# An encoder layer whose last tiles are finished another way: a reordered tail, and four row tiles whose residual is added by an accumulating transfer

## The chip, the cores and the metric

The kernel runs on one core of one Trainium2 chip. The metric is the device time of one execution in microseconds (us). Three runs of the kernel before gave 1161.38, 1163.57 and 1164.84 us, a median of 1163.57. One further execution was profiled: it took 1163.79 us, of which the profile's span covers 1162.1.

## The reference

One layer of a transformer-like encoder over 1024 tokens of width 1024, in float32:

```
h = x + rms_norm(Mix(rms_norm(x, g_pre_mix)), g_post_mix)
u = rms_norm(h, g_pre_mlp)
f = square(relu(u @ w_ff_in))          # 1024 x 4096
y = f @ w_ff_out                        # 1024 x 1024
out = h + rms_norm(y, g_post_mlp)       # y * rsqrt(mean(y*y) + EPS) * g + h
```

Mix is one input projection, three groups of heads (stick-breaking attention, a gated recurrence, windowed attention) and an output projection. The change touches only the last line: how `h` is kept meanwhile and how the last norm and the last addition are made.

## The kernel before

The tokens lie in 8 tiles of 128 rows (`TOK`); `y[:, i, :]` is tile i, 128 partitions by 1024 columns of float32 (512 KB). After Mix, `y` holds `h`. The MLP needs `y`'s space, so SyncE writes each tile of `h` to a DRAM tensor `h_dram` (`h_spill` in the profile) around 483 to 506 us, and reads all of it back into `h_back` at 1050 us, 4 MB in one transfer.

The MLP is cut into 8 stages (`STAGES`): even ones make hidden columns, odd ones add their share to `y`. A stage is 7 products of 512x512x512 blocks (Strassen-like; `P1, P2, P6, P5, P7, P3, P4`, in this order). Each float32 product is three passes of rounded parts: ScalarE (ACT) rounds the operands to `a_op` and `b_op` (`round_operands`), VectorE (DVE) makes what is left of them (`rest_operands`), TensorE (PE) multiplies, and DVE adds the product in PSUM (`ps`) to its one or two blocks of `y` (`evict_output`). In the last stage P2 ends the block of tiles 0 to 3 and columns 0 to 511, P7 ends the block of tiles 4 to 7 and columns 512 to 1023, P3 ends tiles 0 to 3, columns 512 to 1023, and P4 ends tiles 4 to 7, columns 0 to 511. P4 is made tile by tile, so that each of its four tiles can be taken when it is done (`last_tile_sum`).

The tail that follows, all written out by hand in the order of each engine's queue:

- ACT squares and sums half rows (`late_squares`): eight halves that are done early into `sumsq_b`, then for each tile the other half into `sumsq`, followed by Ln and Exp that give a first `rs0` of the tile's reciprocal root.
- DVE multiplies every half row by the gain (`gained_half`, 16 of them into `out_gained`), turns `sumsq_b` into `var_b`, adds P4's tiles, improves the root (`final_rsqrt`, four small instructions for one to four tiles) and makes `y = out_gained * rstd + h_back` (`final_tile`, 8 of them).
- SyncE's queue (SP) sends each finished tile to `out`, 512 KB each, and waits for all of them.
- GpSimd (POOL) does nothing after 500 us.

`out_gained` lies over the weight blocks `wq21`, `wq12` and so on; `junk_late`, the squares' unused output, lies over `a_sum`.

Of the kernel before, what the change touches and what calls it, by code (L numbers as in the profile page):

```python
# [19 lines left out]
ALU = mybir.AluOpType  # L20
ACT = mybir.ActivationFunctionType
AX_X = mybir.AxisListType.X

P = 128
BANK = 512
# [13 lines left out]
TOK = S // P  # L39
# [24 lines left out]
PRODUCTS = 7  # L64
# [19 lines left out]
def encoder_layer(nc, x, g_pre_mix, w_in, conv_w, conv_b, lru_wa, lru_ba, lru_wx, lru_bx,  # L84
# [5 lines left out]
    with ExitStack() as ctx:  # L90
# [16 lines left out]
        def sem(name):  # L107
            return ctx.enter_context(nc.semaphore(name))
# [137 lines left out]
        half_done, product_done = sem("half_done"), sem("product_done")  # L246
        act_evicted, dve_evicted = sem("act_evicted"), sem("dve_evicted")
        f_relu, f_ready, sums_ready = sem("f_relu"), sem("f_ready"), sem("sums_ready")
        var_b_ready = sem("var_b_ready")
        h_loaded, out_gain_done, out_ready, out_stored = (  # L250
            sem("h_loaded"), sem("out_gain_done"), sem("out_ready"), sem("out_stored"))
        act_step, dve_step, pool_step = sem("act_step"), sem("dve_step"), sem("pool_step")
# [124 lines left out]
        def halves(s, i):  # L377

            return 2 * (PRODUCTS * s + i) + 2
# [17 lines left out]
        def dve_reads(n):  # L397

            count = 0
            for s, i in (divmod(m, PRODUCTS) for m in range(n)):  # L400
                if i in (P2, P3, P4, P7):
                    count += 2
                if s % 2 and s > 1 and i in (P1, P6, P5, P7):
                    count += 2
            return count
# [25 lines left out]
        def _(sp):  # L431
# [89 lines left out]
            sp.dma_start(wq11[:, :, :], block_of(0, 0, 0)).then_inc(wq_loaded[0], 16)  # L521
            for i in range(TOK):
                sp.wait_ge(h_ready, i + 1)
                sp.dma_start(h_dram[P * i:P * (i + 1), :], y[:, i, :]).then_inc(h_stored[i // 4], 16)
                if i == 3:
                    sp.dma_start(wq21[:, :, :], block_of(0, 1, 0)).then_inc(wq_loaded[2], 16)
                if i == 7:
                    sp.dma_start(wq12[:, :, :], block_of(0, 0, 1)).then_inc(wq_loaded[1], 16)
                    sp.dma_start(wq22[:, :, :], block_of(0, 1, 1)).then_inc(wq_loaded[3], 16)
# [12 lines left out]
            for half in range(2):  # L542
                sp.wait_ge(h_stored[half], 16 * 4)
            sp.wait_ge(a_lo_ready, halves(STAGES - 2, P4))
            sp.dma_start(h_back[:, :, :], h_dram.rearrange("(i p) d -> p i d", p=P))\
                .then_inc(h_loaded, 16)
            for i in range(TOK):
                sp.wait_ge(out_ready, i + 1)
                sp.dma_start(out[0, P * i:P * (i + 1), :], y[:, i, :]).then_inc(out_stored, 16)
            sp.wait_ge(out_stored, 16 * TOK)  # L550


        N_CONST_LOADS = 10
# [2 lines left out]
        def _(pool):  # L556
# [80 lines left out]
            for i in range(TOK - 1):  # L637
                pool.wait_ge(y_added, banks_out(3) + 2 * (i + 1))
                nc.gpsimd.tensor_tensor(y_gained[:, i, :], y[:, i, :], rs_row[:, :], ALU.mult)\
                    .then_inc(y_gain_done, 1)  # L640

        @block.tensor
# [381 lines left out]
        def _(act):  # L1026
# [268 lines left out]
            def turned(half):  # L1295

                for k in range(0, KD, 2):
                    t = KD * half + k
                    act.wait_ge(xt_ready, 2 * KD + t + 1)
                    nc.scalar.activation(ut[:, half, k, :], ps[:, 4 + t % 4, :], ACT.Copy,  # L1300
                                         scale=g_pre_mlp_c[:, k:k + 1]).then_inc(ut_by_act, 1)
# [75 lines left out]
            def relu_squared(s, i):  # L1377

                f = {P2: f11, P7: f22, P3: f12, P4: f21}[i]
                act.wait_ge(dve_evicted, dve_reads(PRODUCTS * s + i + 1))  # L1380
                n_relu[0] += 1
                nc.scalar.activation(f[:, :, :], f[:, :, :], ACT.Relu).then_inc(f_relu, 1)
                act.wait_ge(f_relu, n_relu[0])
                nc.scalar.activation(f[:, :, :], f[:, :, :], ACT.Square).then_inc(f_ready, 1)
# [10 lines left out]
            normed(1)  # L1395
            round_operands(1)
            turned(1)
            for n in range(N_PRODUCTS):
                s, i = divmod(n, PRODUCTS)
                if n:  # L1400
                    evict(n - 1)
                    if n + 1 < N_PRODUCTS:
                        round_operands(n + 1)
                if s % 2 == 0 and i in (P6, P3, P4):
                    relu_squared(s, i - 1 if i != P6 else P2)
                if s % 2 and i == P1:
                    relu_squared(s - 1, P4)

            def late_squares(i, c, total):

                n_squares[0] += 1
                act.wait_ge(sumsq_ready, n_squares[0] - 1)
                nc.scalar.activation(junk_late[:, BANK * c:BANK * (c + 1)],
                                     y[:, i, BANK * c:BANK * (c + 1)], ACT.Square,
                                     accum_out=total[:, i:i + 1]).then_inc(sumsq_ready, 1)

            last = PRODUCTS * (STAGES - 1)
            act.wait_ge(a_lo_ready, halves(STAGES - 1, P4))
            act.wait_ge(dve_evicted, dve_reads(last + P7 + 1))
            for i in range(TOK):  # L1420
                late_squares(i, i // 4, sumsq_b)
            act.wait_ge(sumsq_ready, n_squares[0])
            for i in range(TOK):
                act.wait_ge(dve_evicted, dve_reads(last + P3) + i // 2 + 1 if i < 4
                            else dve_reads(last + P3 + 1) + i - 3)
                late_squares(i, 1 - i // 4, sumsq)
                act.wait_ge(var_b_ready, 1)
                act.wait_ge(sumsq_ready, n_squares[0])
                after(nc.scalar.activation(ln_var[:, i:i + 1], sumsq[:, i:i + 1], ACT.Ln,
                                           scale=1.0 / D, bias=var_b[:, i:i + 1]))  # L1430
                nc.scalar.activation(rs0[:, i:i + 1], ln_var[:, i:i + 1], ACT.Exp, scale=-0.5)\
                    .then_inc(rs0_ready, 1)


        @block.vector
        def _(dve):
# [436 lines left out]
            def evict(n):  # L1873
# [3 lines left out]
                else:  # L1877
                    evict_hidden(n, s, i)


            SUMS_AT = (("S1", "T2", "S2"), ("T3",), ("S3",), ("S4",), ("T4",), (), ("T1",))

# [7 lines left out]
            for n in range(N_PRODUCTS):  # L1890
                s, i = divmod(n, PRODUCTS)
                if n:
                    if i != P2:
                        rest_operands(n + 1, [0])
                    evict(n - 1)
                    rest_operands(n + 1, range(2) if i == P2 else [1])
                for name in SUMS_AT[i]:
                    if name == "T1":
                        if s + 1 < STAGES:
                            block_sum(s + 1, name)  # L1900
                    elif name != "S1" or s % 2:
                        block_sum(s, name)


            def gained_half(i, c):

                cols = slice(BANK * c, BANK * (c + 1))
                nc.vector.tensor_tensor(out_gained[:, i, cols], y[:, i, cols], rs_row[:, cols],  # L1908
                                        ALU.mult).then_inc(out_gain_done, 1)

            def final_tile(i):

                nc.vector.scalar_tensor_tensor(out=y[:, i, :], in0=out_gained[:, i, :],  # L1913
                                               scalar=rstd[:, i:i + 1], in1=h_back[:, i, :],
                                               op0=ALU.mult, op1=ALU.add).then_inc(out_ready, 1)
# [12 lines left out]
            def last_tile_sum(t):  # L1928

                n = N_PRODUCTS - 1  # L1930
                dve.wait_ge(product_done, 2 * n + t + 1)
                n_evicted[0] += 1
                nc.vector.tensor_tensor(y[:, 4 + t, 0:BANK], y[:, 4 + t, 0:BANK],
                                        ps[:, 4 * (n % 2) + t, :], ALU.add)\
                    .then_inc(dve_evicted, 1)
                dve.wait_ge(dve_evicted, n_evicted[0])
                gained_half(4 + t, 0)

            dve.wait_ge(rows_loaded, 32)
            dve.wait_ge(sumsq_ready, 4 * TOK)  # L1940
            nc.vector.tensor_scalar(var_b[:, :], sumsq_b[:, :], 1.0 / D, EPS, ALU.mult, ALU.add)\
                .then_inc(var_b_ready, 1)
            dve.wait_ge(dve_evicted, n_evicted[0])
            for i in range(4):
                gained_half(i, 0)
            for i in range(4, TOK):
                gained_half(i, 1)
            for i in range(4):
                gained_half(i, 1)
            last_tile_sum(0)  # L1950
            last_tile_sum(1)
            dve.wait_ge(h_loaded, 16)
            dve.wait_ge(var_b_ready, 1)
            final_rsqrt(range(4), 1)
            dve.wait_ge(out_gain_done, 14)
            final_tile(0)
            final_tile(1)
            last_tile_sum(2)
            final_rsqrt((4, 5), 2)
            final_tile(2)  # L1960
            last_tile_sum(3)
            final_tile(3)
            final_tile(4)
            final_tile(5)
            for i in (6, 7):
                final_rsqrt((i,), i - 3)
                if i == 6:
                    dve.wait_ge(out_gain_done, 16)
                final_tile(i)


# [20 lines left out]
```

## Time and profile before

| | |
|---|---|
| median of three runs | 1163.57 us (1161.38 to 1164.84) |
| the profiled execution | 1163.79 us, span 1162.1 us |
| PE busy | 1082.9 us, 93% of the span |
| DVE busy | 808.2 us, 70% |
| ACT busy | 574.1 us, 49% |
| POOL busy | 76.2 us, 7% |
| chain that ended last | PE 84%, DVE 8%, ACT 4%, issue 2%, DMA 1% |
| stores of `out` | 8 of 512 KB, median 2.7 us from issue to landing |

The shares are means over the whole span. What the change is worth is read from the last 35 us, where the engines take turns.

### The profile page before, as it was taken

How to read it: one execution, taken by the hardware profiler on the slowest of the kernel's cores; microseconds unless marked ns; L12 is line 12 of the kernel's file. 1: busy time of each engine (PE TensorE's matmuls, PEld its weight loads, DVE VectorE, ACT ScalarE, POOL GpSimd, SP SyncE). 2: the span in 40 equal slices, each digit the busy share in tenths (PEclk: the TensorE clock that was granted, in tenths of full speed). 3: DMA queues.
4: the chain of work that ended last, by engine and by line, in shares of the span. 5: the costliest groups of instructions: out<-in, count | busy, mean ns of one | idle time of the engine just before them, and what ended most of it. 6: DMA issues, size and time to landing. Idle time of an engine off the chain costs nothing.

```text
span 1162.1 us, 12115 instructions
## 1 busy us (share of the span) xinstructions
PE 1082.9 (93%) x4844; PEld 844.6 (73%) x4844; DVE 808.2 (70%) x767; ACT 574.1 (49%) x705; POOL 76.2 (7%) x69
## 2 busy tenths in 40 slices
PE   6999999997899999849999999999999999999992
PEld 5777777875535458637888888878888878888781
DVE  2536657655464645767778777789876898867988
ACT  6313433357464540475665546654366533467443
POOL 0004113201101000400000000000000000000000
PEclk9999999978899999978999999999999999999996
DMA  7211112110000122160130311301303013025003
GB/s 220 76 46 37 37 37 73 37 37 1 1 1 1 36 108 93 48 225 1 37 109 1 111 34 37 109 1 38 108 1 143 2 37 109 1 76 214 1 1 144
DMA packets 44624, 70.44 MB, mean 61 GB/s; under 512 B 10228, under 2 KB 19736, under 8 KB 44568
## 3 DMA queue, kind: packets, MB, share of 16 engines
q1 hardware_dynamic: 43528, 69.66, 17.6%
q8 instruction: 39, 0.64, 0.2%
q10 hardware_dynamic: 1040, 0.00, 0.1%
q14 instruction: 17, 0.14, 0.0%
HBM read 61.27 MB, written 8.39 MB: 60 GB/s over the span
## 4 chain that ended last, share of the span: by engine, by line
PE 84%; DVE 8%; ACT 4%; issue 2%; DMA 1%; SPq 1%; DVEq 0%; ACTq 0%
PE ps L648 25%; PE ps L652 24%; PE ps L650 24%; PE ps L864 2%; PE ps L877 1%; PE ps L724 1%; PE ps L832 1%; PE ps L892 1%; PE ps L787 1%; DVE sb_e L1658 1%; ACT sb_e L1233 1%; DVE y L1913 1%; DMA g_pre_mix_c<-in_g_pre_mix 1%; ACT sb_w L1213 1%; DVE out_gained L1908 1%
## 5 line engine op out<-in xcount | busy, mean ns | idle before, releaser
L648 PE MATMUL ps<-a_op,b_op 128*128 128x512 f32 x448 | 175.9, 393 | 5.4 <-DVE b_op L1800 4.5
L648 PE MATMUL ps<-b_op,a_op 128*128 128x512 f32 x448 | 174.6, 390 | 2.7 <-issue 2.7
L650 PE MATMUL ps<-a_op,b_op 128*128 128x512 f32 x448 | 175.6, 392 | 0.0
L652 PE MATMUL ps<-a_op,b_op 128*128 128x512 f32 x448 | 175.4, 391 | 0.0
L652 PE MATMUL ps<-b_op,a_op 128*128 128x512 f32 x448 | 174.3, 389 | 0.0
L650 PE MATMUL ps<-b_op,a_op 128*128 128x512 f32 x448 | 174.3, 389 | 0.0
L648 PE MATMUL ps<-act_hi,w_hi 128*128 128x512 f32 x288 | 114.8, 399 | 3.2 <-DVE w_lo L1450 3.2
L1347 ACT CAST a_op<-f 128x1024 fp32r<-128x1024 f32 x56 | 58.8, 1050 | 118.9 <-PE ps L652 78.8
L1800 DVE TENSOR_TENSOR b_op<-wq,b_op 128x1024 fp32r<-128x1024 f32 x96 | 116.9, 1218 | 0.0
L650 PE MATMUL ps<-act_lo,w_hi 128*128 128x512 f32 x288 | 112.8, 392 | 0.0
L652 PE MATMUL ps<-act_hi,w_lo 128*128 128x512 f32 x288 | 112.8, 392 | 0.0
L648 PEld LDWEIGHTS ps<-a_op,b_op 128*128 128x128 f32 x448 | 84.9, 189 | 24.0 <-issue 6.3
L1793 DVE TENSOR_TENSOR a_op<-f,a_op 128x1024 fp32r<-128x1024 f32 x56 | 68.4, 1222 | 47.7 <-ACT a_op L1347 47.7
L1351 ACT CAST b_op<-wq 128x1024 fp32r<-128x1024 f32 x96 | 100.6, 1048 | 0.0
L648 PEld LDWEIGHTS ps<-b_op,a_op 128*128 128x128 f32 x448 | 84.1, 188 | 21.3 <-issue 4.1
L652 PEld LDWEIGHTS ps<-a_op,b_op 128*128 128x128 f32 x448 | 84.9, 189 | 17.9
L650 PEld LDWEIGHTS ps<-a_op,b_op 128*128 128x128 f32 x448 | 84.8, 189 | 17.6
L652 PEld LDWEIGHTS ps<-b_op,a_op 128*128 128x128 f32 x448 | 84.1, 188 | 17.6
L650 PEld LDWEIGHTS ps<-b_op,a_op 128*128 128x128 f32 x448 | 84.1, 188 | 17.3
L1347 ACT CAST a_op<-ut 128x1024 fp32r<-128x1024 f32 x32 | 33.6, 1051 | 76.0 <-PE ps L652 75.4
L648 PEld LDWEIGHTS ps<-act_hi,w_hi 128*128 128x128 f32 x288 | 54.5, 189 | 16.5 <-issue 5.4
L1040 ACT CAST w_hi<-stage 128x1024 fp32r<-128x1024 f32 x26 | 26.1, 1047 | 77.3 <-PE ps L652 72.2
(190 smaller groups left out, 1756.4 us busy)
## 6 DMA issues: line engine op xcount, KB each, us to landing
wq<-in_w_ff_in SPq DMA_DIRECT2D x16, 1024.0 KB, 5.5
wq<-in_w_ff_out SPq DMA_DIRECT2D x16, 1024.0 KB, 5.1
stage<-in_w_in SPq DMA_DIRECT2D x18, 512.0 KB, 4.3
y<-in_x SPq DMA_DIRECT2D x4, 1024.0 KB, 10.0
stage<-in_w_out SPq DMA_DIRECT2D x8, 512.0 KB, 3.8
h_spill<-y SPq DMA_DIRECT2D x8, 512.0 KB, 3.0
h_back<-h_spill SPq DMA_DIRECT2D x1, 4096.0 KB, 15.5
out<-y SPq DMA_DIRECT2D x8, 512.0 KB, 2.7
```

Source lines behind the costliest of these rows:

```text
L648: nc.tensor.matmul(dst, stat[0], mov[0], start=first, stop=False, skip_group_check=chained)
L650: nc.tensor.matmul(dst, stat[0], mov[1], start=False, stop=False, skip_group_check=chained)
L652: return nc.tensor.matmul(dst, stat[1], mov[0], start=False, stop=last, skip_group_check=chained)
L724: mm = nc.tensor.matmul(ps[:, 4 + 2 * m + half, :], gate_w[:, m, c, :], work[:, 0, BANK * half:BANK * (half + 1)], start=True, stop=True)
L787: mm = nc.tensor.matmul(ps[CHUNK * e:CHUNK * (e + 1), b + i // 4, P * (i % 4) + off:P * (i % 4 + 1)], qt[rows, CHUNK * c:CHUNK * (c + 1)], ...
L832: mm = nc.tensor.matmul(ps[:, 2 * (s % 2) + a, c0:], sk_t[p][rows, P * j:P * (j + 1)], sq_t[p][rows, BANK * half + c0:BANK * (half + 1)], ...
L864: mm = nc.tensor.matmul(ps[:, 2 * (s % 2) + a, c0:], neg_tri[:, :], sb_l[:, s % 2, a, c0:], start=False, stop=True, skip_group_check=True)
L1040: nc.scalar.copy(w_hi[:, slot, 1024 * s:1024 * (s + 1)], stage[:, s, :])\
L1347: nc.scalar.copy(a_op[:, half % A_SLOTS, 0], src).then_inc(a_hi_ready, 1)
L1351: nc.scalar.copy(b_op[:, (half + 3) % B_SLOTS, 0], src).then_inc(b_hi_ready, 1)
L1793: nc.vector.tensor_tensor(slot[:, 1], a_source(s, i, kk), slot[:, 0].bitcast(F32), ALU.subtract)\
L1800: nc.vector.tensor_tensor(slot[:, 1], src, slot[:, 0].bitcast(F32), ALU.subtract).then_inc(b_lo_ready, 1)
```

## The change

Three things are altered.

1. For tiles 0 to 3 `h` is written straight to the rows of `out` and not to `h_dram`. `h_back` loads tiles 4 to 7 only. At the end ACT scales `out_gained` of tiles 0 to 3 by `rstd` into `y`, and POOL issues for each of them a transfer that adds `y` to the rows of `out` (`accum_op=ALU.add`). DVE's `final_tile` remains for tiles 4 to 7.
2. ACT squares tiles 0 to 3 (columns 0 to 511) before it rounds P4's operands, and tiles 4 to 7 (columns 512 to 1023) after them.
3. DVE gains tiles 0 to 3 (columns 0 to 511) ahead of P3's eviction, and all of P4's tiles are taken before the first root.

```
@@ sync
-                sp.dma_start(h_dram[P * i:P * (i + 1), :], y[:, i, :]).then_inc(h_stored[i // 4], 16)
+                rows = slice(P * i, P * (i + 1))
+                sp.dma_start(out[0, rows, :] if i < 4 else h_dram[rows, :], y[:, i, :])\
+                    .then_inc(h_stored[i // 4], 16)
...
-            sp.dma_start(h_back[:, :, :], h_dram.rearrange("(i p) d -> p i d", p=P))\
+            sp.dma_start(h_back[:, 4:, :], h_dram[BANK:, :].rearrange("(i p) d -> p i d", p=P))\
                 .then_inc(h_loaded, 16)
-            for i in range(TOK):
-                sp.wait_ge(out_ready, i + 1)
+            for i in range(4, TOK):
+                sp.wait_ge(out_ready, i - 3)
                 sp.dma_start(out[0, P * i:P * (i + 1), :], y[:, i, :]).then_inc(out_stored, 16)
@@ gpsimd
+            pool.wait_ge(h_stored[0], 16 * 4)
+            for i in range(4):
+                pool.wait_ge(scaled_ready, i + 1)
+                pool.dma_start(out[0, P * i:P * (i + 1), :], y[:, i, :], accum_op=ALU.add)\
+                    .then_inc(out_added, 16)
+            pool.wait_ge(out_added, 16 * 4)
@@ scalar
+                if n == last + P7:
+                    act.wait_ge(a_lo_ready, halves(STAGES - 1, P7))
+                    act.wait_ge(dve_evicted, dve_reads(last + P2 + 1))
+                    for i in range(4):
+                        late_squares(i, 0, sumsq_b)
+                if n == last + P3:
+                    act.wait_ge(dve_evicted, dve_reads(last + P7 + 1))
+                    for i in range(4, TOK):
+                        late_squares(i, 1, sumsq_b)
...
+            for i in range(4):
+                act.wait_ge(rstd_ready, 8)
+                act.wait_ge(out_gain_done, 10 + i)
+                nc.scalar.activation(y[:, i, :], out_gained[:, i, :], ACT.Copy,
+                                     scale=rstd[:, i:i + 1]).then_inc(scaled_ready, 1)
@@ vector
+                if n == N_PRODUCTS - 2:
+                    dve.wait_ge(rows_loaded, 32)
+                    dve.wait_ge(b_lo_ready, halves(STAGES - 1, P4))
+                    for i in range(4):
+                        gained_half(i, 0)
```

On VectorE, from the remainders of P4's operands (`b_op` at L1800) to the end of the first root, the queue holds in the kernel before:

```order
600 L1800 TENSOR_TENSOR b_op<-wq_74,b_op 128x1024
601 L1836 TENSOR_TENSOR y<-y,ps 128x2x512 x2
602 L1941 TENSOR_SCALAR var_b<-sumsq_b 128x8
603 L1908 TENSOR_TENSOR out_gained<-y,rs_row 128x512 x12
604 L1933 TENSOR_TENSOR y<-y,ps 128x512
605 L1908 TENSOR_TENSOR out_gained<-y,rs_row 128x512
606 L1933 TENSOR_TENSOR y<-y,ps 128x512
607 L1908 TENSOR_TENSOR out_gained<-y,rs_row 128x512
```

and in the changed kernel, where the same operations have the lines 1824, 1860, 1907, 1962 and 1972:

```order
600 L1824 TENSOR_TENSOR b_op<-wq_74,b_op 128x1024
601 L1907 TENSOR_TENSOR out_gained<-y,rs_row 128x512 x4
602 L1860 TENSOR_TENSOR y<-y,ps 128x2x512 x2
603 L1907 TENSOR_TENSOR out_gained<-y,rs_row 128x512 x4
604 L1972 TENSOR_SCALAR var_b<-sumsq_b 128x8
605 L1962 TENSOR_TENSOR y<-y,ps 128x512
606 L1907 TENSOR_TENSOR out_gained<-y,rs_row 128x512 x5
607 L1962 TENSOR_TENSOR y<-y,ps 128x512
```

Eight of the half rows now stand ahead of `var_b`, four of them ahead of P3's eviction (the `y<-y,ps` of 128x2x512), and one tile of P4 is taken before the last four early halves.

On ScalarE, from the rounding of P3's last operand (`b_op<-wq_76`) to the first Ln, the queue holds before, with what each waits for:

```order
521 L1351 CAST b_op<-wq_76 128x1024 [waits product_done,wq_loaded3]
522 L1347 CAST a_op<-f_67 128x1024 [waits product_done,f_ready]
523 L1351 CAST b_op<-wq_74 128x1024 [waits half_done,sums_ready]
524 L1347 CAST a_op<-f_67 128x1024 [waits half_done,f_ready]
525 L1351 CAST b_op<-wq_74 128x1024 [waits product_done,sums_ready]
526 L1413 ACTIVATE junk_late,sumsq_b<-y 128x512 [waits sumsq_ready,dve_evicted,a_lo_ready]
527 L1413 ACTIVATE junk_late,sumsq_b<-y 128x512 [waits sumsq_ready] x7
```

and now:

```order
521 L1363 CAST b_op<-wq_76 128x1024 [waits product_done,wq_loaded3]
522 L1414 ACTIVATE junk_late,sumsq_b<-y 128x512 [waits sumsq_ready,dve_evicted,a_lo_ready]
523 L1414 ACTIVATE junk_late,sumsq_b<-y 128x512 [waits sumsq_ready] x3
524 L1359 CAST a_op<-f_67 128x1024 [waits product_done,f_ready]
525 L1363 CAST b_op<-wq_74 128x1024 [waits half_done,sums_ready]
526 L1359 CAST a_op<-f_67 128x1024 [waits half_done,f_ready]
527 L1363 CAST b_op<-wq_74 128x1024 [waits product_done,sums_ready]
528 L1414 ACTIVATE junk_late,sumsq_b<-y 128x512 [waits sumsq_ready,dve_evicted]
```

Four squares stand in front of the four casts of P4's operands instead of behind them.

## Rows read from the trace of the kernel before

**Rows 1.** Busy time of each engine in two stretches of the span.
```profile
core 0: us, PE busy (x) PEld busy (x) DVE busy (x) ACT busy (x) POOL busy (x), PEclk, DMA share, GB/s
1100.00:1140.00 40.00, 40.00 (x177) 32.86 (x175) 35.83 (x36) 21.15 (x43) 0.00 (x0) 1.00 0.00 1
1140.00:1162.10 22.10, 0.06 (x1) 0.00 (x0) 18.32 (x34) 4.86 (x16) 0.00 (x0) 0.58 0.47 190
```

**Rows 2.** Timeline of VectorE: start, duration in us, line, what; idle before in brackets.
```profile
1121.76 4.60 DVE L1836 TENSOR_TENSOR y<-y,ps 128x1024 f32<-128x1024 f32 x4
...
1127.42 1.22 DVE L1800 TENSOR_TENSOR b_op<-wq,b_op 128x1024 fp32r<-128x1024 f32 x1
1128.55 2.34 DVE L1836 TENSOR_TENSOR y<-y,ps 128x1024 f32<-128x1024 f32 x2
1133.65 0.17 DVE L1941 TENSOR_SCALAR var_b<-sumsq_b 128x8 f32<-128x8 f32 x1 [2.75 <-ACT junk_late L1413]
1133.73 7.31 DVE L1908 TENSOR_TENSOR out_gained<-y,rs_row 128x512 f32<-128x512 f32 x12
1140.95 0.68 DVE L1933 TENSOR_TENSOR y<-y,ps 128x512 f32<-128x512 f32 x1
...
1142.28 0.68 DVE L1933 TENSOR_TENSOR y<-y,ps 128x512 f32<-128x512 f32 x1
...
1143.60 0.15 DVE L1921 SCALAR_TENSOR_TENSOR var<-sumsq,var_b 128x4 f32<-128x4 f32 x1
...
1144.38 2.48 DVE L1913 SCALAR_TENSOR_TENSOR y<-out_gained,rstd,h_back 128x1024 f32<-128x1024 f32 x2
1146.78 0.68 DVE L1933 TENSOR_TENSOR y<-y,ps 128x512 f32<-128x512 f32 x1
...
1157.73 1.28 DVE L1913 SCALAR_TENSOR_TENSOR y<-out_gained,rstd,h_back 128x1024 f32<-128x1024 f32 x1
```

**Rows 3.** Timeline of ScalarE, the last operands and the first sums.
```profile
1113.91 1.05 ACT L1351 CAST b_op<-wq 128x1024 fp32r<-128x1024 f32 x1
1118.39 1.05 ACT L1347 CAST a_op<-f 128x1024 fp32r<-128x1024 f32 x1 [3.44 <-PE ps L652]
...
1127.53 0.63 ACT L1413 ACTIVATE junk_late<-y 128x512 f32<-128x512 f32 x1 [1.69 <-DVE a_op L1793]
...
1128.29 0.63 ACT L1413 ACTIVATE junk_late<-y 128x512 f32<-128x512 f32 x1
...
1134.47 0.29 ACT L1429 ACTIVATE ln_var<-sumsq,var_b 128x1 f32<-128x1 f32 x1
...
1134.91 0.62 ACT L1413 ACTIVATE junk_late<-y 128x512 f32<-128x512 f32 x1
...
1136.15 0.62 ACT L1413 ACTIVATE junk_late<-y 128x512 f32<-128x512 f32 x1
```

**Rows 4.** Timeline of TensorE: first and last of product P4's 48 matmuls.
```profile
1129.02 0.39 PE L648 MATMUL ps<-b_op,a_op 128*128 128x512 f32 x1
...
1139.67 0.39 PE L652 MATMUL ps<-b_op,a_op 128*128 128x512 f32 x1
```

**Rows 5.** The stores of `out`: ns of an issue, first and last start, landing.
```profile
L549 SPq DMA_DIRECT2D out<-y x8: 332/333/356, 1145.7 to 1159.0; - x8
...
DMA to landing us min/median/max: 2.6/2.7/2.8
```

**Rows 6.** The stretch of the stores, columns as in rows 1.
```profile
1145.70:1162.10 16.40, 0.00 (x0) 0.00 (x0) 12.82 (x23) 2.44 (x8) 0.00 (x0) 0.50 0.63 256
```

**Rows 7.** Four loads of 512 KB from DRAM behind each other.
```profile
L499 SPq DMA_DIRECT2D x_again<-in_x x4: 347/432/433, 424.8 to 426.1; - x4
...
DMA to landing us min/median/max: 3.6/5.2/6.7
```

**Rows 8.** Timelines of POOL and VectorE where the two meet.
```profile
478.85 2.42 POOL L639 TENSOR_TENSOR y_gained<-y,rs_row 128x1024 f32<-128x1024 f32 x1 [0.31 <-DVE y L1749]
...
478.88 2.40 DVE L1457 SCALAR_TENSOR_TENSOR rs_t<-rs 128x2 f32<-128x2 f32 x1
```

More of the change, by code:

```diff
@@ L248, in encoder_layer @@
         f_relu, f_ready, sums_ready = sem("f_relu"), sem("f_ready"), sem("sums_ready")
-        var_b_ready = sem("var_b_ready")
+        var_b_ready, scaled_ready, out_added = (
+            sem("var_b_ready"), sem("scaled_ready"), sem("out_added"))
         h_loaded, out_gain_done, out_ready, out_stored = (
@@ L544, in _ @@
             sp.wait_ge(a_lo_ready, halves(STAGES - 2, P4))
-            sp.dma_start(h_back[:, :, :], h_dram.rearrange("(i p) d -> p i d", p=P))\
+            sp.dma_start(h_back[:, 4:, :], h_dram[BANK:, :].rearrange("(i p) d -> p i d", p=P))\
                 .then_inc(h_loaded, 16)
-            for i in range(TOK):
-                sp.wait_ge(out_ready, i + 1)
+            for i in range(4, TOK):
+                sp.wait_ge(out_ready, i - 3)
                 sp.dma_start(out[0, P * i:P * (i + 1), :], y[:, i, :]).then_inc(out_stored, 16)
-            sp.wait_ge(out_stored, 16 * TOK)
+            sp.wait_ge(out_stored, 16 * 4)
         N_CONST_LOADS = 10
@@ L1397, in _, with late_squares @@
             turned(1)
+            def late_squares(i, c, total):
+                n_squares[0] += 1
+                act.wait_ge(sumsq_ready, n_squares[0] - 1)
+                nc.scalar.activation(junk_late[:, BANK * c:BANK * (c + 1)],
+                                     y[:, i, BANK * c:BANK * (c + 1)], ACT.Square,
+                                     accum_out=total[:, i:i + 1]).then_inc(sumsq_ready, 1)
+            last = PRODUCTS * (STAGES - 1)
             for n in range(N_PRODUCTS):
@@ L1407, in _ @@
                     relu_squared(s - 1, P4)
[L1409 to L1421, printed above, removed]
+                if n == last + P7:
[7 more added lines that the diff above has]
+                        late_squares(i, 1, sumsq_b)
             act.wait_ge(sumsq_ready, n_squares[0])
@@ L1878, in evict, with gained_half @@
                     evict_hidden(n, s, i)
+            def gained_half(i, c):
+                cols = slice(BANK * c, BANK * (c + 1))
+                nc.vector.tensor_tensor(out_gained[:, i, cols], y[:, i, cols], rs_row[:, cols],
+                                        ALU.mult).then_inc(out_gain_done, 1)
             SUMS_AT = (("S1", "T2", "S2"), ("T3",), ("S3",), ("S4",), ("T4",), (), ("T1",))
@@ L1902, in _ @@
                         block_sum(s, name)
[L1905 to L1909, printed above, removed]
+                if n == N_PRODUCTS - 2:
[3 more added lines that the diff above has]
+                        gained_half(i, 0)
             def final_tile(i):
@@ L1937, in last_tile_sum @@
                 gained_half(4 + t, 0)
-            dve.wait_ge(rows_loaded, 32)
+            dve.wait_ge(dve_evicted, n_evicted[0])
+            for i in range(4, TOK):
+                gained_half(i, 1)
             dve.wait_ge(sumsq_ready, 4 * TOK)
@@ L1942, in _ @@
                 .then_inc(var_b_ready, 1)
[L1943 to L1947, printed above, removed]
+            last_tile_sum(0)
             for i in range(4):
                 gained_half(i, 1)
-            last_tile_sum(0)
-            last_tile_sum(1)
+            for t in range(1, 4):
+                last_tile_sum(t)
             dve.wait_ge(h_loaded, 16)
@@ L1954, in _ @@
             final_rsqrt(range(4), 1)
[L1955 to L1958, printed above, removed]
+            dve.wait_ge(out_gain_done, 16)
             final_rsqrt((4, 5), 2)
-            final_tile(2)
-            last_tile_sum(3)
-            final_tile(3)
             final_tile(4)
@@ L1966, in _ @@
                 final_rsqrt((i,), i - 3)
-                if i == 6:
-                    dve.wait_ge(out_gain_done, 16)
                 final_tile(i)
```

## The prediction

> **What bounds the kernel now.** I read the windows first. From 1100 to 1140 us TensorE is busy for 40.00 of 40.00 us, and in the last 22.1 us it does nothing, while VectorE is busy for 18.32 us and the DMA engines for 47% [rows 1]. So there is a stretch that TensorE bounds, which the change could only harm, and a tail of 22 us in which something may be won. The last product starts at 1129.02 and its 48 matmuls, 0.227 us apart, end about 1140.0; its first tile is done after 12 of them, near 1131.9 [rows 4].
>
> Next the timeline of VectorE [rows 2]. It goes from one thing to the next, with one hole: after P3's eviction (1128.55 plus 2.34) it waits 2.75 us for ScalarE's squares before `var_b`. Then come 12 half rows in 7.31 us (0.60 each), so that P4's first tile, done at 1131.9, is taken only at 1140.95. A P4 tile with its half row costs 1.33 us (1140.95 to 1142.28), a root 0.78 us (1143.60 to 1144.38), a final tile 1.20 us (1144.38 to 1146.78 for two). The last final tile starts at 1157.73 and ends at 1159.01. Its store is issued at 1159.0 and lands 2.7 us later [rows 5], 1161.7; the span ends at 1162.1, 0.4 us on. VectorE's queue sets the end, and TensorE has nothing to do with it after 1140.
>
> **The front of the change: does it touch TensorE?** ScalarE has four more squares ahead of P4's casts. A square with its accumulator costs 0.76 us (1127.53 to 1128.29), four cost 3.0. They can start when the cast at 1113.91 ends, about 1114.9, and end at 1117.9. The next cast started at 1118.39 only because TensorE released its slot then, after 3.44 us of idle time [rows 3]. The squares fit with 0.4 us to spare; P4's operands are ready at 1128.64 for a product that starts at 1129.02, another 0.4 us. I cost this at nothing. Without that cover the price would be the 3.0 us of the squares. The four half rows that VectorE gains early stand behind P4's last remainder, so no operand waits for them; they push P3's eviction, which no matmul waits for any more. For tiles 0 to 3 `h` goes to `out` in place of `h_dram`, the same bytes at the same time: nothing. `h_back` halves to 2 MB at 1050 us, with 90 us to spare: nothing. SP's queue has only the stores of tiles 4 to 7 behind it, POOL's nothing at all.
>
> **VectorE's queue after the change**, from 1128.55, all with the durations above:
> - four half rows 2.4, P3's eviction 2.3, four half rows 2.4: 1135.7. The squares of `sumsq_b` are done at 1126.4 + 3.0 = 1129.4, since P7's eviction ends at 1126.36 [rows 2], so the hole of 2.75 us is gone.
> - `var_b` 0.1: 1135.8. One P4 tile 1.3, four half rows 2.4, three P4 tiles 4.0: 1143.5. All four P4 tiles are ready by 1140.1, so none is waited for.
> - the roots of tiles 0 to 3 and of 4 and 5, 1.6: 1145.1. Two final tiles 2.4, the first ending at 1146.4; then twice a root and a final tile, 4.0: 1151.5.
> The last store would be issued at 1151.5 and not at 1159.0, 7.5 us earlier: 2.75 for the hole and 4.8 for four final tiles that VectorE no longer makes. With these stores alone the span would end at 1151.5 + 2.7 + 0.4 = 1154.6.
>
> **ScalarE's queue.** The first Ln waits for `var_b`, 1135.9, and with its Exp takes 0.44 us (1134.47 to 1134.91). Each further tile takes 1.24 us (1134.91 to 1136.15) [rows 3]; seven of them end at 1145.1. Then the four scaled copies of 128x1024. The nearest row is the cast of this size, 1.05 us; they are done at 1146.1, 1147.1, 1148.0 and 1149.0. The accumulating transfers can begin at 1146.2, as early as SP's first store (1146.4).
>
> **The transfers.** This is what I expect to set the end. Before, 8 stores of 512 KB were busy for 63% of 16.40 us, 10.3 us, 1.29 us each [rows 6]; a store lands after 2.7 us, so 1.4 us are fixed. They were spread over 13.3 us, and VectorE set the pace. Now all eight are asked for within 5.3 us, so they queue behind each other on the same 16 DMA engines. An accumulating transfer also has to fetch the rows of `out`. No row shows one, so I bound it:
> - below: 1.29 us, if fetching and adding cost the engines nothing beyond the store. All eight then need 8 x 1.29 = 10.3 us, and the span ends at 1146.4 + 1.4 + 10.3 + 0.4 = 1158.5, 3.6 us less than before. So even this bound gives back half of what VectorE saves.
> - the store and a load one after the other on the engines: of four loads, issued from 424.8 to 426.1, the first lands after 3.6 us (428.4) and the last after 6.7 us (432.8) [rows 7], 1.47 us for each further one. The transfer costs 1.29 + 1.47 = 2.76 us, and the eight need 4 x 1.29 + 4 x 2.76 = 16.2 us: 1146.4 + 1.4 + 16.2 + 0.4 = 1164.4.
> - above: nothing overlaps, each reads its rows (3.6 us to the landing of a lone load) and then stores them (2.7), 6.3 us, four in a row from 1146.2: 1171.4, with the 0.4 us 1171.8; if SP's four stores find no gap between them, 5.2 us more, 1177.0.
> I take the middle one: the bytes that pass each engine are two reads and one write, and the engines were already moving some 400 GB/s whenever they were busy (256 GB/s at 63% [rows 6]).
>
> The Trainium skill has a rule for this sum. In "Collectives: The Full Stack", section "The bandwidth ceiling: the fold count and why AG ≠ RS ≠ AR", an add in the DMA engines is said to take two source reads on one ring, and reduce-scatter to run 1.93 times slower than a copy for that reason alone. By that figure the sum would be 4 x 1.29 + 4 x 2.49 = 15.1 us, an estimate, and the span 1163.3. No row here shows it.
>
> **POOL.** It has to make and issue the transfers; no row shows what an issue costs there. SP's takes 0.33 us [rows 5]; the longest POOL instruction seen beside VectorE is 2.42 us, and a small VectorE instruction beside it took 2.40 us in place of 0.16 [rows 8]. If every issue held VectorE up so, its last store would come 9.6 us later, at 1161.1, and land with the 0.4 us at 1164.2. That is where the transfers end anyway, so it adds nothing to the sum, but it takes away the chance of the lower bound. I take about 1 us an issue, hidden behind the transfers under way.
>
> **The sum.** The span goes from 1162.1 to 1164.4, 2.3 us more. Against its own time of 1163.79 that is 1166.1; the median of the runs is 0.2 us below that time, so I say 1165.8.
>
> **The rivals.** A measurement of this kernel can tell about 0.3%, 3.5 us, from no change.
> - *The added read is free.* For it: the rows of `out` come from DRAM and the tile from SBUF, two ways that might run side by side. Against it: the engines stood near 400 GB/s in the stores and have no spare room that a row shows. Span 1158.5, time 1160.0, just over 0.3% faster. Chance 0.20.
> - *The transfers are dearer than their bytes,* since read, add and write follow each other with their latencies exposed. For it: a load lands after 3.6 us of which only 1.5 are bytes [rows 7], and rows of 4 KB leave little to overlap if each waits for its own reads. Against it: the four loads behind each other did overlap. Halfway between the middle and the upper bound each costs about 4.5 us, and the span ends at 1146.4 + 1.4 + 5.2 + 18.0 + 0.4 = 1171.4, time 1173. It decides (slower by 3.5 us) from 3.1 us a transfer, only 0.3 above my price. Chance 0.33.
> - *The squares are late and TensorE waits.* The two margins of 0.4 us [rows 2 to 4] are thin. If the four squares started only when P4's first cast is due (1118.39), the cast, VectorE's remainders behind it and all of VectorE's queue would move by 3.0 us; TensorE would wait 2.6 of them and the transfers would start 3.0 us later: span 1167.4, time 1169. It decides from the 0.4 us that the squares have. Against it: everything they wait for was done by 1114.9. Chance 0.05.
> - My forecast, the end set by eight transfers at 2.8 us for an accumulating one: chance 0.42.
>
> **How the numbers follow.** Faster 0.20 from the first rival. Slower 0.37: the second, most of the third, and little of the forecast. Same 0.43. The forecast's own range is 1163 to 1167. The range of eight in ten has the free read at its lower end, 1159.5, and goes up to 1174.5, just above the second rival's middle, which leaves its upper half outside.
>
> **What the profile would show.** VectorE's idle time before `var_b` under 0.2 us, and its last final tile ending near 1151.5. ScalarE's first Ln near 1136.0 and four copies from 1145.1. TensorE's last matmul at 1139.7 as before. DMA busy nearly throughout from 1147 to the end, and the chain ending in a transfer of POOL, not in a final tile. POOL's transfers landing 5 to 12 us after their issue, the last after all of SP's. If the DMA engines stand idle for part of that time, latency and not bytes sets the price, and I am wrong toward slower; if an accumulating transfer landed 3 us after its issue, I am wrong toward faster.

## The result, and the profile after

The changed kernel takes 1166.96 us (median of 7 runs, 1165.99 to 1168.49) against 1163.62 us of the kernel before (7 runs beside it, 1161.38 to 1165.02). The ratio is 1.0029 with a 95% interval of 1.0019 to 1.0038: 3.3 us slower, just inside the 0.3% that was called no change, and clear of 1.000. The forecast was 1165.8 us. The profiled execution has a span of 1165.2 us, 3.1 us more than before; forecast were 2.3.

The windows of the changed kernel, to be held against [rows 1]:

```profile
core 0: us, PE busy (x) PEld busy (x) DVE busy (x) ACT busy (x) POOL busy (x), PEclk, DMA share, GB/s
1140.00:1165.20 25.20, 0.09 (x1) 0.00 (x0) 11.08 (x26) 8.97 (x22) 3.74 (x4) 0.58 0.67 166
1146.60:1164.50 17.90, 0.00 (x0) 0.00 (x0) 4.86 (x11) 2.90 (x3) 3.74 (x4) 0.50 0.95 234
1100.00:1140.00 40.00, 40.00 (x177) 32.84 (x175) 38.41 (x40) 20.72 (x42) 0.00 (x0) 1.00 0.00 1
```

VectorE has 7.2 us less to do in the tail (11.08 for 18.32), and yet the tail is 3.1 us longer. From 1146.6 to 1164.5 the DMA engines are busy for 95% of the time. TensorE's stretch is as before, 40.00 of 40.00 us.

VectorE's timeline of the changed kernel, which answers to [rows 2]:

```profile
1127.45 1.22 DVE L1824 TENSOR_TENSOR b_op<-wq,b_op 128x1024 fp32r<-128x1024 f32 x1
1128.77 2.50 DVE L1907 TENSOR_TENSOR out_gained<-y,rs_row 128x512 f32<-128x512 f32 x4
1131.18 2.35 DVE L1860 TENSOR_TENSOR y<-y,ps 128x1024 f32<-128x1024 f32 x2
1133.56 2.50 DVE L1907 TENSOR_TENSOR out_gained<-y,rs_row 128x512 f32<-128x512 f32 x4
1135.98 0.16 DVE L1972 TENSOR_SCALAR var_b<-sumsq_b 128x8 f32<-128x8 f32 x1
1136.05 0.68 DVE L1962 TENSOR_TENSOR y<-y,ps 128x512 f32<-128x512 f32 x1
...
1145.31 2.48 DVE L1942 SCALAR_TENSOR_TENSOR y<-out_gained,rstd,h_back 128x1024 f32<-128x1024 f32 x2
...
1150.46 1.28 DVE L1942 SCALAR_TENSOR_TENSOR y<-out_gained,rstd,h_back 128x1024 f32<-128x1024 f32 x1
```

No row carries an idle time: the hole of 2.75 us ahead of `var_b` is gone, and the last final tile ends at 1151.74. ScalarE's timeline around the four squares that were moved and its last copies, against [rows 3]:

```profile
1117.15 0.63 ACT L1414 ACTIVATE junk_late<-y 128x512 f32<-128x512 f32 x1
1117.69 0.19 ACT L1414 ACTIVATION_READ_ACCUMULATOR junk_late<-y 128x1 f32 x1
1118.42 1.05 ACT L1359 CAST a_op<-f 128x1024 fp32r<-128x1024 f32 x1 [0.55 <-PE ps L664]
...
1136.17 0.29 ACT L1446 ACTIVATE ln_var<-sumsq,var_b 128x1 f32<-128x1 f32 x1 [2.97 <-DVE var_b L1972]
...
1145.25 4.25 ACT L1455 ACTIVATE y<-out_gained,rstd 128x1024 f32<-128x1024 f32 x4
```

The cast of P4's first operand waits for TensorE still, 0.55 us: the squares fitted in front of it. Then the transfers of `out` in the changed kernel, from the view by tile and from the DMA view of 1140 to 1165.2 (queue, packets, MB, share of 16 engines), against [rows 5]:

```profile
L552 SPq DMA_DIRECT2D out<-y x4: 332/341/357, 1146.6 to 1151.8; - x4
L651 POOL DMA_DIRECT2D out<-y x4: 978/1087/1196, 1147.0 to 1149.8; - x4
```

```profile
q0 software_dynamic: 576, 2.10, 45.1%
q1 hardware_dynamic: 576, 2.10, 22.1%
issues: line engine op xcount, KB each, median us to landing
out<-y SPq DMA_DIRECT2D x4, 512.0 KB, 8.5
out<-y POOLq DMA_DIRECT2D x4, 512.0 KB, 10.9
```

q0 is POOL's queue. The same 2.10 MB take 45.1% of 25.2 us there, 11.4 us or 2.84 us a transfer, and 22.1%, 5.6 us or 1.39 us a transfer, in SyncE's. A store of SyncE's that landed in 2.7 us now takes 8.5 in the median; the engines are full while it is under way. POOL's transfers land 7.2 to 14.6 us after their issue.

One measure serves all the runs below. The time ahead of the last product differs by up to 5.3 us from one profiled execution to another (the last matmul started between 1135.5 and 1140.8 us), so I give the **tail**, from the start of the last matmul to the end of the span. It was 1162.1 - 1139.67 = 22.4 us before and 1165.2 - 1139.70 = 25.5 us after.

### The profile page after: what moved, and what is told of

Read it like the earlier page. It is cut to its first block, busy times and chain, and to the rows that moved or that the text cites. A ratio compares the mean times of both kernels' runs of the same rounds, so it can differ in the third digit from the quotient of the medians.

```text
span 1165.2 us, 12121 instructions
## 1 busy us (share of the span) xinstructions
PE 1081.7 (93%) x4844; PEld 845.1 (73%) x4844; DVE 803.5 (69%) x763; ACT 577.8 (50%) x709; POOL 79.6 (7%) x73
## 4 chain that ended last, share of the span: by engine, by line
PE 83%; DVE 8%; ACT 4%; issue 2%; DMA 1%; SPq 1%; POOL 0%; DVEq 0%; ACTq 0%
PE ps L660 25%; PE ps L664 24%; PE ps L662 24%; PE ps L876 2%; PE ps L736 1%; PE ps L889 1%; PE ps L904 1%; PE ps L799 1%; PE ps L844 1%; DVE out_gained L1907 1%; DVE sb_e L1682 1%; ACT sb_e L1245 1%; DMA g_pre_mix_c<-in_g_pre_mix 1%; DVE ps L1716 1%; PE ps L983 1%
```

## The experiments

Theory A is that of the forecast: the tail is bound by the bytes of eight transfers, and an accumulating one counts twice. What the runs can weigh is the time for which the DMA engines are busy with a transfer; that this time goes by bytes is the forecast's reading of it. The rivals are named in what was expected.

### The reordered queues alone

```
-                sp.dma_start(out[0, rows, :] if i < 4 else h_dram[rows, :], y[:, i, :])
+                sp.dma_start(h_dram[rows, :], y[:, i, :])
...
-                pool.dma_start(out[0, P * i:P * (i + 1), :], y[:, i, :], accum_op=ALU.add)
...
             dve.wait_ge(out_gain_done, 16)
+            for i in range(4):
+                final_tile(i)
             final_rsqrt((4, 5), 2)
```

> The reordered queues of VectorE and ScalarE alone: h goes to its own DRAM tensor for all tiles, VectorE makes all eight final tiles (0 to 3 right after the roots of 4 tiles), SyncE stores all eight, POOL issues nothing. Theory A (the tail of the changed kernel is bound by the bytes of eight transfers, an accumulating one worth two): VectorE ends 4.8 us later than in the changed kernel, 1156.5, the last store lands 2.7 us later, the span ends at 1159.6, 2.5 us below before (ratio 0.998). Rival B (the transfers bind however they are made, since all are asked for at once): 1162 or more.

Measured: 1161.17 us (7 runs), ratio to before 0.9978 [0.9966, 0.9989]; tail 1157.8 - 1137.89 = 19.9 us, 2.5 us below before, as expected. Its stores by the view by tile:

```profile
L552 SPq DMA_DIRECT2D out<-y x8: 332/333/357, 1144.0 to 1154.8; - x8
...
DMA to landing us min/median/max: 2.6/2.7/2.9
```

Eight stores whose issues are spread over 10.8 us still land in 2.7 us each, so here VectorE sets the pace and not the transfers; rival B falls for this spacing. The changed kernel asks for its eight within 5.2 us, and the next run shows what eight plain ones do then. The reordering is worth 2.5 us, and with the accumulating transfers on top the tail is 5.6 us worse than without them.

### Plain transfers from POOL

```
-                pool.dma_start(out[0, P * i:P * (i + 1), :], y[:, i, :], accum_op=ALU.add)\
+                pool.dma_start(out[0, P * i:P * (i + 1), :], y[:, i, :])\
```

> POOL's four transfers are plain stores and add nothing, so the residual of tiles 0 to 3 is left out of the output; all else as in the changed kernel. Theory A (the second read is what an accumulating transfer costs): each is worth 1.3 to 1.4 us of the engines, the eight need 11 us, and the span ends at 1159, 6 us below the changed kernel. Rival C (the cost is the path through POOL: its issue of 1.1 us and the software queue): the transfers still land 7 to 15 us after their issue and the span stays at 1165.

Measured: 1161.10 us (10 runs), ratio 0.9975 [0.9966, 0.9984]; tail 1158.6 - 1139.25 = 19.4 us, 6.1 us below the changed kernel. The DMA view of 1142 to 1175 (busy tenths in 40 slices, then the queues) and the view by tile of this kernel:

```profile
DMA  0000009899999999999000000000000000000000
...
q0 software_dynamic: 576, 2.10, 16.2%
q1 hardware_dynamic: 576, 2.10, 16.1%
```

```profile
L651 POOL DMA_DIRECT2D out<-y x4: 531/534/748, 1146.6 to 1149.3; - x4
...
DMA to landing us min/median/max: 2.7/6.1/8.1
```

Through POOL or through SyncE a plain store costs the engines the same, 16.2% or 16.1% of 33 us, 1.3 us each. POOL's queue is not what costs; rival C falls. Taking away the add alone takes away 6.1 us. In step with it POOL's issue falls from 1.09 to 0.53 us; the engines are full behind the issues in both kernels.

The run shows one thing more: even eight plain transfers bind when they are asked for this closely. VectorE's last final tile ends at 1151.31, and its store alone would have landed 2.7 us later, with a span of 1154.4; the span is 1158.6, and the engines are busy at nine tenths or more in nearly every slice until then. That is the lower bound of the prediction (1158.5), measured. So the 4.8 us that VectorE saves by leaving four final tiles to ScalarE and the DMA engines are worth only 0.5 us of tail against the reordered queues (19.4 for 19.9) and nothing in the medians (1161.10 for 1161.17), before any add is paid for.

### The accumulating transfers alone

The last store of tile 7 follows when they have landed, and tiles 4 to 6 are not stored:

```
+                if i == 7:
+                    sp.wait_ge(out_added, 16 * 4)
                     sp.dma_start(out[0, P * i:P * (i + 1), :], y[:, i, :]).then_inc(out_stored, 16)
-            sp.wait_ge(out_stored, 16 * 4)
+            sp.wait_ge(out_stored, 16)
```

> The changed kernel without the tail's stores from SyncE, but for one of tile 7 after all four accumulating transfers have landed: tiles 4 to 6 are left out of the output. The four accumulating transfers have the DMA engines to themselves, issued about 1 us apart. Theory A (bytes): the engines are busy for 4 x 2.84 = 11.4 us, and the last lands about 13 us after the first is issued, each 2.8 us after the one ahead. Rival F (the share of 2.84 us was the crowding by SyncE's stores): 1.5 us apart, all landed within 8 us.

This kernel ran once, 1165.96 us. Its DMA view of 1142 to 1175 (busy tenths and GB/s in 40 slices, then the queues) and the view by tile:

```profile
DMA  0000000009789999999999207700000000000000
GB/s 0 0 0 0 0 0 0 0 0 99 114 164 233 189 209 213 204 213 218 204 213 218 50 0 313 323 0 0 0 0 0 0 0 0 0 0 0 0 0 0
...
q0 software_dynamic: 576, 2.10, 34.8%
```

```profile
L653 POOL DMA_DIRECT2D out<-y x4: 980/1090/1201, 1148.0 to 1150.8; - x4
...
DMA to landing us min/median/max: 2.6/7.3/10.3
```

The engines are busy for 34.8% of 33 us, 11.5 us or 2.87 us each, with nothing beside them. The last one, issued at 1150.8, lands 10.3 us later at 1161.1, 13.1 us after the first was issued. Theory A expected 11.4 and 13; rival F falls. While the engines are full they deliver 189 to 233 GB/s of stored bytes a slice, about half of the 372 to 407 in the full slices of the run with plain transfers.

### Each accumulating transfer behind the landing of the one ahead

```
                 pool.wait_ge(scaled_ready, i + 1)
+                if i:
+                    pool.wait_ge(out_added, 16 * i)
```

> As the run with the accumulating transfers alone, but each is issued only when the one ahead has landed: tiles 4 to 6 are left out of the output. It shows the landing of a lone accumulating transfer. Theory A: the fixed part of a store (1.4 us) and 2.8 us of bytes, with POOL's issue of 1.1 us about 5 us from issue to landing. Rival G (read, add and write follow each other with latencies exposed): 6.3 us and more beside the issue, 7.4 us or above, with the engines busy for much of it.

This kernel ran once, 1175.21 us. Its view by tile, the DMA slices of 1142 to 1175, and two of the three later issues in POOL's timeline:

```profile
L655 POOL DMA_DIRECT2D out<-y x4: 865/865/1052, 1147.5 to 1164.9; - x4
...
DMA to landing us min/median/max: 2.6/5.2/5.5
```

```profile
DMA  0000000095993009799200798900094992059000
GB/s 0 0 0 0 0 0 0 0 79 94 189 218 55 0 0 79 109 184 223 40 0 0 79 154 169 223 10 0 0 79 70 218 228 40 0 209 412 15 0 0
```

```profile
1153.36 0.86 POOL L655 DMA_DIRECT2D out<-y  x1 [4.82 <-DMA out<-y]
1159.09 0.86 POOL L655 DMA_DIRECT2D out<-y  x1 [4.86 <-DMA out<-y]
```

A lone one lands 5.2 to 5.5 us after its issue; expected about 5, and 7.4 or more by rival G, which falls. The slices show a smaller part of truth in it: each transfer starts at 70 to 154 GB/s and reaches some 220 only in its second half. By the same view POOL's queue takes 40.4% of 33 us for four, 3.3 us each, so a lone one keeps the engines busy for longer than one in a row.

### The squares back behind the casts

```
-                if n == last + P7:
-                    act.wait_ge(a_lo_ready, halves(STAGES - 1, P7))
-                    act.wait_ge(dve_evicted, dve_reads(last + P2 + 1))
-                    for i in range(4):
-                        late_squares(i, 0, sumsq_b)
...
+                if n == last + P4:
+                    act.wait_ge(a_lo_ready, halves(STAGES - 1, P4))
+                    act.wait_ge(dve_evicted, dve_reads(last + P7 + 1))
+                    for i in range(TOK):
+                        late_squares(i, i // 4, sumsq_b)
```

> The changed kernel with ScalarE's eight early squares back behind P4's casts, as before the change. VectorE reaches var_b at 1136.0 in any case, and the eight squares end near 1133.6, so I expect no hole and no difference: 1165.2 in the span, ratio to the changed kernel 1.000. Rival D (moving the squares is what closed the hole of 2.75 us): the hole comes back and everything behind it moves by up to 2.8 us.

Measured: 1167.91 us (6 runs), ratio to before 1.0030 [1.0018, 1.0041], for 1.0029 of the changed kernel; tail 1166.1 - 1140.51 = 25.6 us for 25.5. VectorE of this kernel:

```profile
1134.38 2.50 DVE L1903 TENSOR_TENSOR out_gained<-y,rs_row 128x512 f32<-128x512 f32 x4
1136.79 0.17 DVE L1968 TENSOR_SCALAR var_b<-sumsq_b 128x8 f32<-128x8 f32 x1
```

No idle time ahead of `var_b`; rival D falls. The new place of the squares gives nothing here.

### The two reorderings, each without the other

First the reordered queues alone as above, with the squares back behind the casts by the edit just shown.

> The reorder alone, with ScalarE's eight early squares left where they were before the change. VectorE reaches var_b near 1136 in the time of the kernel before, after the squares end (1133.6), so VectorE's new order alone closes the hole: span 1159.5, ratio to before 0.998, as with both. Rival: the squares' new place is needed, ratio 1.000.

Measured: 1161.45 us (12 runs), ratio 0.9976 [0.9965, 0.9987], tail 1155.3 - 1135.47 = 19.8 us. VectorE goes from four half rows (from 1129.33, 2.50 us) to `var_b` at 1131.75 without idle time.

Then the kernel before with nothing but ScalarE's squares moved ahead, the first part of that edit turned round.

> The kernel before with only ScalarE's squares moved ahead. They end at 1129.5, before VectorE is done with P3's eviction (1130.9), so the hole of 2.75 us closes this way too: ratio 0.998. The two reorderings are two ways to one gain, not two gains. Rival: VectorE meets the next wait (for ScalarE's roots or TensorE's P4 tiles) and gets less, ratio 0.999 or above.

Measured: 1161.86 us (11 runs), ratio 0.9979 [0.9970, 0.9988], tail 1158.2 - 1138.63 = 19.6 us. VectorE there:

```profile
1127.51 2.35 DVE L1841 TENSOR_TENSOR y<-y,ps 128x1024 f32<-128x1024 f32 x2
1129.78 0.17 DVE L1946 TENSOR_SCALAR var_b<-sumsq_b 128x8 f32<-128x8 f32 x1
1129.89 7.32 DVE L1913 TENSOR_TENSOR out_gained<-y,rs_row 128x512 f32<-128x512 f32 x12
```

The hole closes in this way too. Each reordering alone gives what both give, 2.5 to 2.8 us: one hole, two ways to fill it.

### Fewer tiles added

The loops that scale, add and load back go over 2 tiles, or 1, in place of 4, and VectorE makes the other final tiles.

```
-            for i in range(4):
+            for i in range(2):
                 pool.wait_ge(scaled_ready, i + 1)
...
             dve.wait_ge(out_gain_done, 16)
+            for i in range(2, 4):
+                final_tile(i)
             final_rsqrt((4, 5), 2)
```

> The changed kernel with accumulating transfers for tiles 0 and 1 only; VectorE makes the final tiles 2 to 7. Theory A: VectorE ends at 1154.1; the transfers need 6 x 1.33 + 2 x 2.84 = 13.7 us of the engines from 1146, and the span ends near 1161.3, between the changed kernel and the reorder alone. Rival E (an accumulating transfer costs its latency, not bytes, and the latencies run side by side): VectorE's last store decides, 1157.2.

Measured: 1164.39 us (11 runs), ratio 1.0000 [0.9991, 1.0009]; span 1161.8, tail 22.1 us. Theory A expected 1161.3, rival E 1157.2; E falls. The two accumulating transfers take 19.1% of 33 us in the DMA view, 3.15 us each and not 2.84, and all eight transfers 14.2 us for the expected 13.7.

> The changed kernel with an accumulating transfer for tile 0 only. VectorE ends 3.6 us later than in the changed kernel and 1.2 us earlier than with the reorder alone. By bytes the transfers need 7 x 1.33 + 2.84 = 12.2 us of the engines from the first store on, which ends with the last store of the reorder alone, so theory A expects no gain over it: ratio 0.997 to 0.998. If the accumulating transfer fitted into gaps of the stores, 1.2 us better: 0.9967.

Measured: 1161.59 us (12 runs), ratio 0.9984 [0.9975, 0.9992]; tail 1161.4 - 1140.78 = 20.6 us, 0.7 us above the reorder alone. No gain over it, as theory A said; whether it is a loss the intervals cannot tell (0.9966 to 0.9989 there). The one accumulating transfer takes 10.5% of 33 us, 3.5 us.

So with 0, 1, 2 and 4 tiles added the tail is 19.9, 20.6, 22.1 and 25.5 us, and VectorE's part of it is shorter each time (from the start of the last matmul to the end of the last final tile 16.8, 15.6, 14.4 and 12.0 us).

## Why the prediction was right, point by point

- **The front of the change costs nothing:** shown. The squares ended 0.55 us before TensorE released the slot, and TensorE kept 40.00 of 40.00 us.
- **VectorE's queue:** right in each place. Forecast `var_b` at 1135.8, first final tile from 1145.1, last one done at 1151.5; seen 1135.98, 1145.31, 1151.74. The hole is gone. That the new order of VectorE suffices for it, and the squares' place adds nothing, the prediction did not say; it put the hole's end down to the squares, and three runs show that either is enough.
- **ScalarE's queue:** first Ln forecast 1135.9, seen 1136.17; copies from 1145.1, seen 1145.25, together 4.25 us for the forecast 3.9. POOL's first issue began at 1147.03, 0.8 us later than forecast; what that cost is not shown.
- **The transfers set the end:** shown by the run without the add (6.1 us shorter) and by the counts of tiles. The price of an accumulating transfer was forecast as 2.76 us and measured as 2.84, and 2.87 alone. The price was right, its reason was weaker: "two reads and one write" against one read and one write of a plain store would give 1.5 times 1.29, or 1.9 us, if each counted alike, while the sum took a whole load and a whole store. That a load from another stretch fitted so well was partly luck. Busy time is not bytes either: a lone transfer keeps the engines busy for seven to nine tenths of its first slice while they deliver 79 GB/s. So the runs show the engine time of an accumulating transfer, not what fills it; no run has fewer bytes or other rows.
- **The Trainium skill's rule** (two source reads on one ring, in "Collectives: The Full Stack", section "The bandwidth ceiling: the fold count and why AG ≠ RS ≠ AR") is stated there for collectives in a ring of three ranks or more, with a measured ratio of 1.93. Here the ratio to a plain store is 2.84 / 1.39 = 2.04 beside the stores, and 2.87 against 1.34 of the plain run, 2.14; the page's figure was a little low for this transfer, and the measurement decides. The runs say what an accumulating transfer costs, not through which ring the second read goes; that stays the page's account.
- **The term that was too small** is the sum of the engines' work: forecast 16.2 us, seen 67.2% of 25.2 us, 16.9. Of the 0.7 us, 0.4 lies in plain stores that cost 1.39 in the crowd and not 1.29, and 0.3 in the added ones. The first store was issued 0.2 us later than forecast. Together 0.9 us, which is the difference of 3.1 and 2.3 within what can be read. The measured 1166.96 us lies at the very top of the forecast's own range of 1163 to 1167.
- **The rivals:** the free read is refuted by the added transfers alone. The dearer one (4.5 us each) is refuted in the crowd and even by lone transfers (3.3 us of the engines, 3.5 us with one tile added). It had a point for few: these lie above the 3.1 us from which the prediction would have called it, and only four in a row bring the mean to 2.84. POOL's issue took 1.09 us for the forecast 1; no VectorE instruction was held up beside it (final tiles 1.28 us, the small ones of the roots 0.15 to 0.16 us, as before).
- **The signs:** POOL's last transfer did land after SyncE's last, but they took 7.2 to 14.6 us and not 5 to 12. The profile's chain follows instructions and stops at VectorE's last final tile, so it does not show the end in a transfer; some 12 us of full DMA engines behind it do.

## What to carry to other kernels

When work is moved from an engine to the DMA engines at the end of a kernel, add up all transfers that are then asked for at once, in engine time, and compare the sum with the time until the old end; an accumulating store of these tiles counts for two. Here 4.8 us of VectorE were worth at most 0.5 us once the stores queued, and were paid for with 4 x 1.5 us more of the DMA engines. The gain lay in the free part, the hole of 2.75 us: the version to keep is either reordering without the transfers, 0.998 of the time before.

## What the runs showed of the hardware that was not expected

- POOL issues a plain store of 128x1024 float32 in 0.53 us (one of the four in 0.75) and an accumulating one in 0.87 to 1.2 us. The three accumulating ones issued after VectorE had ended took 0.86 or 0.87 us, those beside its last tiles 0.98 to 1.20. Whether VectorE is the reason is open: the three were also issued singly, on idle DMA engines.
- A lone accumulating transfer starts slowly: 79 GB/s of stored bytes in its first slice of 0.8 us, in which the engines are busy for seven to nine tenths, against 209 GB/s at five tenths and then 412 of the plain store in the same trace. Why is open; no run separates the reads from the adding.
- The time ahead of the tail (some 1140 us) differs by up to 5.3 us between profiled executions of kernels whose matmuls are the same there. A single span says little on a change of 3 us in the tail; the tail's own length does.
